# Pairing experts j and j+16, and summing each token's lower-block row ahead of the last scatter

## What is computed

```
def hier_moe(h, ...):                       # h: RMSNorm(x), 1088 x 1024
    pg = softmax(h @ w_rg + b_rg);  p_grp, g_sel = top_k(pg, 1)       # one of 4 groups
    le = einsum('nd,gde->nge', h, w_re) + b_re, of group g_sel        # 8 experts in it
    pe = softmax(le);  top_p, top_i = top_k(pe, 2)
    gates = p_grp * (top_p / sum(top_p));  eid = g_sel * 8 + top_i    # 2 of 32 experts
    y[token] += gate * (silu(xb @ w_eg[e]) * (xb @ w_eu[e])) @ w_ed[e]
x = x + hier_moe(rms_norm(x));  y_out = rms_norm(x)
```

## Time and profile before

| | |
|---|---|
| Time, median of 3 runs | 1012.75 us (1012.13 to 1013.37) |
| The profiled execution: its own time | 1013.96 us |
| Its span, first to last instruction | 1012.2 us |
| TensorE busy | 928.2 us (92%) |
| VectorE busy | 840.0 us (83%) |
| ScalarE (ACT) busy | 584.7 us (58%) |
| GpSimd (POOL) busy | 158.8 us (16%) |
| TensorE clock granted, mean | 0.962 |
| HBM read, written | 259.33 MB, 31.38 MB |

### The profile page before, as it was taken

The page is one execution under the profiler, slowest core; times in us unless marked ns, Lnnn a source line. Parts: engine busy times, 40 slices in busy tenths (PEclk is TensorE's granted clock), DMA queues, the critical chain, the costliest instruction groups (busy, mean ns, idle before and its releaser), DMA issues.

```text
span 1012.2 us, 13964 instructions
## 1 busy us (share of the span) xinstructions
PE 928.2 (92%) x4691; PEld 794.1 (78%) x4691; DVE 840.0 (83%) x932; ACT 584.7 (58%) x559; POOL 158.8 (16%) x201
## 2 busy tenths in 40 slices
PE   5999999968999988999999999999999999999900
PEld 5999988857888787788888888888888888888700
DVE  6489997897677676999989898988989898998658
ACT  7311101495232143778788787878878787887432
POOL 1000000000000021222122222212222221222100
PEclk9999999989999978999999999999999999999955
DMA  9421241321323257999999999999999999999776
GB/s 276 121 62 42 65 132 53 133 109 57 135 97 112 86 209 291 317 411 378 387 392 383 397 384 412 391 390 387 384 399 374 395 377 382 387 382 392 275 300 239
DMA packets 70954, 275.69 MB, mean 272 GB/s; under 512 B 16799, under 2 KB 31647, under 8 KB 45257
## 3 DMA queue, kind: packets, MB, share of 16 engines
q1 hardware_dynamic: 61129, 257.41, 67.6%
q0 software_dynamic: 9792, 17.85, 4.6%
HBM read 259.33 MB, written 31.38 MB: 287 GB/s over the span
## 4 chain that ended last, share of the span: by engine, by line
PE 86%; DVE 6%; DMA 3%; issue 2%; ACT 2%; SPq 0%; POOLq 0%; POOL 0%; DVEq 0%; ACTq 0%
PE ps L1163 11%; PE ps L1165 11%; PE ps L1164 11%; PE ps L1182 6%; PE ps L1180 6%; PE ps L1181 6%; PE ps L894 5%; PE ps L895 5%; PE ps L896 5%; PE ps L938 3%; PE ps L1052 3%; PE ps L1054 3%; PE ps L1053 3%; PE ps L1135 3%; DVE arena L1754 2%
## 5 line engine op out<-in xcount | busy, mean ns | idle before, releaser
L1663 DVE TENSOR_TENSOR big<-arena,big 128x2048 fp32r<-128x2048 f32 x128 | 287.1, 2285 | 0.0
L786 ACT ACTIVATE big<-arena 128x2048 fp32r<-128x2048 f32 x128 | 238.1, 1909 | 3.1 <-PE ps L1165 1.4
L1163 PE MATMUL ps<-big,ring 128*128 128x512 f32 x508 | 201.1, 396 | 2.3 <-DVE big L1663 2.3
L1165 PE MATMUL ps<-big,ring 128*128 128x512 f32 x508 | 198.1, 390 | 0.0
L1164 PE MATMUL ps<-big,ring 128*128 128x512 f32 x508 | 197.6, 389 | 0.0
L1663 DVE TENSOR_TENSOR slot_tail<-arena,slot_tail 128x2048 fp32r<-128x2048 f32 x62 | 139.1, 2285 | 0.0
L786 ACT ACTIVATE slot_tail<-arena 128x2048 fp32r<-128x2048 f32 x62 | 115.4, 1918 | 0.0
L1163 PEld LDWEIGHTS ps<-big,ring 128*128 128x128 f32 x508 | 95.4, 188 | 21.7 <-DVE big L1663 3.2
L1165 PEld LDWEIGHTS ps<-big,ring 128*128 128x128 f32 x508 | 95.4, 188 | 20.3
L1164 PEld LDWEIGHTS ps<-big,ring 128*128 128x128 f32 x508 | 95.5, 188 | 18.7
L1180 PE MATMUL ps<-slot_tail,hTr 128*128 128x512 f32 x248 | 99.2, 400 | 0.0
(11 more groups left out here) (251 smaller groups left out, 1424.4 us busy)
## 6 DMA issues: line engine op xcount, KB each, us to landing
arena<-in_w_eg SPq DMA_DIRECT2D x64, 1024.0 KB, 7.9
arena<-in_w_eu SPq DMA_DIRECT2D x64, 1024.0 KB, 9.1
arena<-in_w_ed SPq DMA_DIRECT2D x64, 1024.0 KB, 9.5
arena<-in_x_prompt SPq DMA_DIRECT2D x16, 512.0 KB, 5.1
arena<-y_scratch SPq DMA_DIRECT2D x8, 1024.0 KB, 11.3
arena<-in_w_in SPq DMA_DIRECT2D x12, 512.0 KB, 4.0
arena<-in_conv_band SPq DMA_DIRECT2D x8, 576.0 KB, 4.6
arena<-in_w_out SPq DMA_DIRECT2D x8, 512.0 KB, 5.2
```

The costliest lines, as they stand in the source:

```text
L786: act.activation(we_h[n % SLOTS], raw[n % RAWS], ACT.Copy).then_inc(high_done, 1)
L1163: pe.matmul(out, part_h[b][:, k, :], wh[:, i, :], start=(k == 0), stop=False)
L1165: ins = pe.matmul(out, part_l[b][:, k, :], wh[:, i, :], start=False, stop=(k == KD - 1))
L1663: dve.tensor_tensor(we_l[n % SLOTS], raw[n % RAWS], we_h[n % SLOTS].bitcast(F32), ALU.subtract).then_inc(low_done, 1)
```

## The change

Experts are paired j and j+16: block 2j holds expert j, block 2j+1 expert j+16. The router's weights and biases come from the host as two arrays with columns in block order, and are loaded in two transfers. A token's first row (k = 0) is now that of its lower block, its second row that of the higher one; e_top remembers which block had the larger logit, and the gates are swapped where that is not the first. The gates are worked out behind the last pair's second hidden product. At the end SP loads x2 tiles and first rows as raw slots come free during the last pair, once pair 14 has been scattered; VectorE adds first rows to x2 (add_first) ahead of all combines; second rows are loaded behind the last scatter, 512 KB per tile. ACT's scratch output lies in PSUM, and its table for the root is loaded before it waits.

```diff
+        PLACE = (2, 3, 4, 5, 0, 1, 6, 7, 8)
+        x_in = [arena[:, 2 * p * D:(2 * p + 1) * D] for p in PLACE]
+        y_first = [arena[:, (2 * p + 1) * D:(2 * p + 2) * D] for p in PLACE]
+        y_second = [arena[:, (2 * NT + 1 + s) * D:(2 * NT + 2 + s) * D] for s in range(FB)]
+        junk_f = banks(5, 2)
...
+            sp.dma_start(w_rt[:, :, :], w_router.rearrange("(p k) n -> p k n", p=P)).then_inc(consts_in, 16)
+            sp.dma_start(b_rt[:, :], b_router.partition_broadcast(P)).then_inc(consts_in, 16)
...
             def weights(j, first=False):
-                e = {b: 2 * j + b for b in (-1, 0, 1)}
+                e = {-1: j - 1 + E // 2, 0: j, 1: j + E // 2}
...
+            first_there = sp.value_load(eob[0:1, OVERFLOW + 2:OVERFLOW + 3], min_val=16 * PAIRS, max_val=16 * MAX_PAIRS + 16)
+            ahead = sp.value_load(eob[0:1, OVERFLOW + 3:OVERFLOW + 4], min_val=NP * PAIRS, max_val=NP * MAX_PAIRS + len(LAST))
+            for t in range(4):
+                sp.wait_ge(low_done, ahead + SLOTS + PLACE[t] + 1)
+                load_x2(t)
+            sp.wait_ge(scat[0], first_there)
+            sp.wait_ge(scat[1], first_there)
+            for t in range(4):
+                load_first(t)
+            for t in (4, 5):
+                sp.wait_ge(low_done, over(n_pairs - 1, NP - 2 + PLACE[t]))
+                load_x2(t)
+                load_first(t)
+            sp.wait_ge(piece_used, ahead + NP)
             sp.dma_start(gf_bc, norm_f_g.partition_broadcast(P)).then_inc(gf_in, 16)
-            sp.wait_ge(scat[0], 16 * n_pairs + 16)
-            sp.wait_ge(scat[1], 16 * n_pairs + 16)
+            for t in range(6, NT):
+                load_x2(t)
+                load_first(t)
+            for b in range(2):
+                sp.wait_ge(gath[b], 16 * n_pairs + 16)
+                sp.wait_ge(scat[b], 16 * n_pairs + 16)
             for t in range(FB):
-                load_y2(t)
+                load_second(t)
...
             over_loop(act, over_body)
+            act.activation(warm[:, :], eps[:, :], ACT.Sqrt)
...
-                step(dve.tensor_copy(eid[0:r, t, :], topi[0:r, 1, 0:2]))
+                dve.tensor_copy(e_top[0:r, t:t + 1], topi[0:r, 1, 0:1])
+                step(dve.tensor_copy(pair[0:r, :], topi[0:r, 1, 0:2]))
+                dve.tensor_tensor(eid[0:r, t, 0:1], pair[0:r, 0:1], pair[0:r, 1:2], ALU.min)
+                step(dve.tensor_tensor(eid[0:r, t, 1:2], pair[0:r, 0:1], pair[0:r, 1:2], ALU.max))
...
+                dve.memset(to_next[:, 0:E:2], float(E // 2))
+                step(dve.memset(to_next[:, 1:E:2], 1.0 - E // 2))
+                step(dve.tensor_tensor(cmp_[:, :, :], cmp_[:, :, :], to_next.unsqueeze(1).to_broadcast([1, OVERFLOW, E]),
+                                       ALU.mult))
                 step(dve.tensor_reduce(eob_f[:, 0:OVERFLOW], cmp_[:, :, :], AX_X, ALU.add))
-                step(dve.tensor_scalar(eob_f[:, 0:OVERFLOW], eob_f[:, 0:OVERFLOW], float(E - 1), None, ALU.min))
...
+                pairs, first_rows, ahead = (eob_f[:, OVERFLOW + i:OVERFLOW + i + 1] for i in range(3))
+                step(dve.tensor_scalar(first_rows, pairs, float(PAIRS), None, ALU.is_gt))
+                step(dve.tensor_scalar(ahead, first_rows, float(len(LAST)), None, ALU.mult))
+                step(dve.scalar_tensor_tensor(ahead, pairs, float(NP), ahead, ALU.mult, ALU.add))
+                step(dve.tensor_tensor(first_rows, first_rows, pairs, ALU.add))
+                step(dve.tensor_scalar(first_rows, first_rows, 16.0, None, ALU.mult))
                 step(dve.memset(eob[:, 0:1], E - 1))
-                dve.tensor_copy(eob[:, 1:OVERFLOW + 2], eob_f[:, 0:OVERFLOW + 1]).then_inc(plan_done, 1)
+                dve.tensor_copy(eob[:, 1:OVERFLOW + 4], eob_f[:, 0:OVERFLOW + 3]).then_inc(plan_done, 1)
+            def set_gates():
...
+                step(dve.tensor_tensor(e_top[:, :], e_top[:, :], eid[:, :, 0], ALU.not_equal))
+                step(dve.tensor_tensor(gtmp[:, :, :], gates[:, :, :], e_top[:, :].unsqueeze(1).to_broadcast([P, 2, NT]),
+                                       ALU.mult))
+                step(dve.tensor_tensor(gates[:, :, :], gates[:, :, :], gtmp[:, :, :], ALU.subtract))
+                dve.tensor_tensor(gates[:, 0, :], gates[:, 0, :], gtmp[:, 1, :], ALU.add)
+                step(dve.tensor_tensor(gates[:, 1, :], gates[:, 1, :], gtmp[:, 0, :], ALU.add))
...
             hidden(PAIRS - 1, 1)
+            set_gates()
             hidden_low(PAIRS - 1, 1)
             over_loop(dve, over_body)
+            def add_first(t):
+                r = ROWS[t]
+                dve.wait_ge(f_x[t], 32)
+                dve.scalar_tensor_tensor(x_in[t][0:r, :], y_first[t][0:r, :], gates[0:r, 0, t:t + 1], x_in[t][0:r, :],
+                                         ALU.mult, ALU.add).then_inc(f_half, 1)
...
+            for t in range(NT):
+                add_first(t)
             for t in range(NT):
                 combine(t)
```

More of the change, by code:

```diff
@@ L62, in trunk_kernel @@
     LB = GROUPS + E
[L63 removed]
+    assert SEQ == 2 * BANK and 2 * IW + PS <= SEQ - PS and SEQ < T and NC + DPOOL // P == KD and NG == NC == 4 and KD == 8 and KF == 4 and PER == 8 and GROUPS == 4 and NBLK % 2 == 0
     VW = CS + SEQ + CS + DEC
@@ L192, in trunk_kernel @@
         FB = 6
[L193 to L196, removed]
+        PLACE = (2, 3, 4, 5, 0, 1, 6, 7, 8)
+        x_in = [arena[:, 2 * p * D:(2 * p + 1) * D] for p in PLACE]
+        y_first = [arena[:, (2 * p + 1) * D:(2 * p + 2) * D] for p in PLACE]
+        gf_bc = arena[:, 2 * NT * D:(2 * NT + 1) * D]
+        y_second = [arena[:, (2 * NT + 1 + s) * D:(2 * NT + 2 + s) * D] for s in range(FB)]
+        assert RAWS * HP == 12 * D
         ident = sb("ident", [P, P])
@@ L229, in trunk_kernel @@
         edif = sb("edif", [P, NT])
+        pair = sb("pair", [P, 2])
+        e_top = sb("e_top", [P, NT])
         gates = sb("gates", [P, 2, NT])
@@ L1745, in _ @@
             hidden(PAIRS - 1, 1)
+            set_gates()
             hidden_low(PAIRS - 1, 1)
             over_loop(dve, over_body)
+            def add_first(t):
+                r = ROWS[t]
+                dve.wait_ge(f_x[t], 32)
+                dve.scalar_tensor_tensor(x_in[t][0:r, :], y_first[t][0:r, :], gates[0:r, 0, t:t + 1], x_in[t][0:r, :],
+                                         ALU.mult, ALU.add).then_inc(f_half, 1)
             def combine(t):
                 r, s = ROWS[t], t % FB
-                dve.wait_ge(f_x[t], 16)
+                dve.wait_ge(f_half, t + 1)
                 dve.wait_ge(f_in[s], 16 * (t // FB + 1))
-                for k in range(2):
-                    dve.scalar_tensor_tensor(x_in[t][0:r, :], y_in[s][0:r, k * D:(k + 1) * D], gates[0:r, k, t:t + 1],
-                                             x_in[t][0:r, :], ALU.mult, ALU.add).then_inc(f_acc, 1)
-                    dve.wait_ge(f_acc, 2 * t + k + 1)
+                dve.scalar_tensor_tensor(x_in[t][0:r, :], y_second[s][0:r, :], gates[0:r, 1, t:t + 1], x_in[t][0:r, :],
+                                         ALU.mult, ALU.add).then_inc(f_acc, 1)
+                dve.wait_ge(f_acc, t + 1)
             def final(t):
@@ L1794, in _ @@
             for g in range(GROUPS):
-                pool.memset(grp[:, g * PER:(g + 1) * PER], float(g))
+                first = g % 2 * 2 * PER + g // 2
+                pool.memset(grp[:, first:first + 2 * PER - 1:2], float(g))
             for i in range(PS):
@@ L1932, in phased_bias, with by_block, router_weights, router_bias @@
     return np.ascontiguousarray(np.tile(conv_dw_b[256:].reshape(-1, 32).T, (4, 1)))
+def by_block(of_experts):
+    import numpy as np
+    n = of_experts.shape[-1]
+    return of_experts[..., [i // 2 + n // 2 * (i % 2) for i in range(n)]]
+def router_weights(w_rg, w_re):
+    import numpy as np
+    w = np.moveaxis(w_re, 0, 1).reshape(w_re.shape[1], -1)
+    return np.ascontiguousarray(np.concatenate([w_rg, by_block(w)], axis=1))
+def router_bias(b_rg, b_re):
+    import numpy as np
+    return np.ascontiguousarray(np.concatenate([b_rg, by_block(b_re.reshape(-1))]))
 _INS = ["x_prompt", "x_sample", "state_pool", "state_conv", "norm1_g", "w_in", "pool_lin", "pool_scale", "conv_dw", "conv_band",
-        "conv_dw_b", "conv_b_ph", "conv_ln_g", "conv_ln_b", "w_out", "b_out", "norm2_g", "w_rg", "b_rg", "w_re", "b_re", "w_eg",
+        "conv_dw_b", "conv_b_ph", "conv_ln_g", "conv_ln_b", "w_out", "b_out", "norm2_g", "w_router", "b_router", "w_eg",
         "w_eu", "w_ed", "norm_f_g"]
@@ L1951 @@
             a = phased_bias(np.asarray(inputs["conv_dw_b"])[0])
+        elif name == "w_router":
+            a = router_weights(np.asarray(inputs["w_rg"])[0], np.asarray(inputs["w_re"])[0])
+        elif name == "b_router":
+            a = router_bias(np.asarray(inputs["b_rg"])[0], np.asarray(inputs["b_re"])[0])
         else:
```

48 lines of the change are left out of this document (22 added, 26 removed).

## The result

| | before | after |
|---|---|---|
| Time, median (lowest to highest), 4 runs each | 1012.92 us (1012.13 to 1013.37) | 1006.96 us (1005.93 to 1008.37) |
| Ratio, 95% interval | | 0.9947 [0.9935, 0.9959] |
| The profiled execution: its own time, span | 1013.96, 1012.2 us | 1007.59, 1005.6 us |
| VectorE busy | 840.0 us | 844.0 us |
| TensorE clock granted, mean | 0.962 | 0.968 |

The kernel became faster by 6.0 us, where 8.7 were forecast. Single executions of one kernel differ by some microseconds, and one reason that the profiles show is TensorE's clock at the first gather of expert rows: in the profiled execution of before it had fallen there (granted clock 0.77 in 375 to 390 us), in that of after it had not (1.00).

What follows compares the result with a forecast made beforehand. TensorE was taken to bound the expert loop, and VectorE's sums behind the last scatter and load the tail. Terms -11.7 + 2.4 + 0.6 = -8.7 gave 1004.0 us from a median of 1012.75, range 1001.0 to 1009.0.

Steps and rivals of the forecast that it cites:

- The sums: Tail behind the last pair: nine of eighteen VectorE sums, 1.30 us each, move ahead of the last scatter; -11.7 us.
- The start of the tail: Tile 0's combine, behind nine first sums, last scatter and one load, starts at 974.5 instead of 972.14; +2.4 us, bounds 972.2 to 979.7.
- the scatter's route: Start of the tail by the last scatter: landed at 970.9, its half-size load behind it, tile 0 ready at 974.4 to 975.6.
- third route: Start of the tail by SP's load queue: 19 units of 1.37 us from 946.9, through at 972.9.
- POOL beside the sums: Last block: POOL's index copy and descriptor writing are slowed by VectorE's first sums running beside them; +0.8 and +1.3 us.
- The load queue's route: Start of the tail by SP's loads: tile 8's first sum ends at 974.2, a second row lands at 974.3.
- The first pair: overflow_plan ahead of low 9: gates and clamp leave, a multiply and small steps come, on TensorE's path; +0.6 us, bounds 0 to 1.2.
- The edits at nothing: Moved gates, routing additions, fewer constant loads and pairing addresses lie under existing idle or busy time; no cost.
- (a): Rival: all transfers hide in the tail, so VectorE's floor of 972.2 decides; 1001.8 us, chance 0.12.
- (b): Rival: the last scatter is starved, landing after 10.1 us, and the tail starts at 979.7; 1009.2 us, chance 0.07.
- (c): Rival: first rows are held back until the last scatter, all eighteen sums stay behind it; 1013.4 us, chance 0.04.
- (d): Rival: experts 32 MB apart are read more slowly, so TensorE waits for weights in every pair; 1020 us, chance 0.05.

Runs made afterwards that it cites:

- the version with all first rows behind: Changed kernel, but all first rows loaded behind the last scatter and summed just ahead of each tile's combine; 1013.09 us, ratio 1.0006 to the kernel before.
- the changed kernel with the plan early: Changed kernel with overflow_plan moved from between low 8 and low 9 to behind rows_low(j, 1) of the first pair; 1003.26 us, ratio 0.9907.

## Why the prediction was right, and where its terms were off

- **The sums**, -11.7: measured -11.70, with one sum per tile in a period of 2.71 us.
- **The start of the tail**, +2.4: measured +6.2, inside the bounds but far from the value taken. The step that was mis-sized is the scatter's route: "The scatter issued at 956.0, among loads, landed after 4.8 instead of 3.20; the last scatter will now meet loads too, so 1.6 more." It was 6.4 more (9.59). The loads beside the scatter of 956.0 ran out while it was under way (q1 moved 0.40 MB in 957 to 958 of that trace, 0.23 in 958 to 959, 0.02 in 959 to 960, and the scatter's packets moved from 958 on); the right rows were the scatters of the weight stream, 10.1, which had been set aside for a rival because "this queue" ends. By the third route of the same section it ends at 972.9, eight microseconds behind the scatter's issue: the two routes were worked out apart, and the first did not use what the second said.
- **POOL beside the sums**, +0.8 and +1.3: the copy took 0.18 as before, the descriptors 1.15 instead of 0.98, +0.17 together. The two terms did not come, which hid part of the error in the scatter.
- **The load queue's route**: near in the trace's time, but too short as well. The last first row was forecast to land at 972.9; it was issued at 955.6 and landed 18.2 later, at 973.8, in an execution that was 1.07 ahead by then. From the first landing (942.03 + 3.5 = 945.5) the 19 units took 1.49 us each, not 1.37. The sum of tile 8 ended at 975.10, 13.12 behind POOL's copy: this route by itself makes +4.0, and the scatter's the remaining 2.17. A second row did not land right behind it, as the forecast had it, but 4.55 us behind a scatter that landed at 972.55.
- **The first pair**, +0.6: the plan took 408.64 - 404.65 = 3.99 instead of 3.50, and the wait 2.15 instead of 1.69, so the instructions were sized well (+0.5, and a wait near the 2.3 named). What was not foreseen is that the clock can fall behind that wait, 1.6 us more in this execution. The profile is nevertheless 1.07 ahead at the last block, since it was 2.95 ahead at the end of TensorE's wait of 0.66 for an earlier low part (402.60 against 405.55): 0.52 of that stood at the last ranks (367.04 against 367.56), the first gather ended TensorE's wait 1.43 earlier (382.26 against 383.69), and from there to the rows of block 1 before took 1.49 longer (7.20 against 5.71) at the fallen clock. Over many executions such differences even out: +0.6 [-0.4, +1.6] in the version with all first rows behind. Why the clock falls in some executions at the first gather and not in others is open: in the six profiles with the fall TensorE had waited 2.86 to 4.08 us for it, in the seven without 0.91 to 3.11.
- **The edits at nothing** cost nothing: the gates end at 951.6, under an idle time of 2.77 that remains ahead of 954.37, the last count ends at 366.38, before TensorE's last ranks at 367.04, and the pairs follow in 35.39 us.
- **The rivals.** (a), all transfers hide: no, VectorE waited 3.91, 0.28, 0.22 and 2.17 us for rows. (b), the last scatter starved: its mechanism is what happened, 9.59 of its 10.1 us; its 1009.2 was too high by 1.4 at the start of the tail (+7.6 against +6.2, 0.8 of it the POOL copy's delay) and by 1.7 ahead of the last block (+0.6 against -1.07). (c) and (d): no; seven of the nine sums lie ahead of the scatter's landing, and the loop is untouched.

In sum -11.7 + 6.2 - 1.07 = -6.6 on the profiled spans, in place of -8.7. The sign rested on the sums, and these were exact. That the time is within the range is in part luck: the start of the tail came by the way of (b), which had a chance of 0.07, 3.8 later than the value taken, and 1.7 of that was given back ahead of the last copy by a difference between two executions that the forecast did not know.

## What to carry to other kernels

Work that is pulled ahead of a latency-bound step is not free if it brings its transfers along: here nine sums saved 11.7 us and the loads for them gave 6.2 back, because the loads took until 973.8 and the scatter that met a filled load queue landed 6 us later, no later with two more loads in the queue. When two routes to one time are worked out, put the result of each into the other before taking the later of them. And a short stall of TensorE can cost more than its length, through the clock that follows it; moving 4 us of VectorE's work from in front of TensorE into a gap it already had was worth 3.7 us, beside the 6.0 of the change itself.

## What was not expected of the hardware

- A scatter's 144 packets stood still for some 4 us behind loads and then took 5 us beside them, against 1 to 2 us and 2 us alone (the queue views above).
- POOL's index copy beside VectorE's sums took 0.18 to 0.19 us in eight profiles and 0.94 and 0.91 in two. In the eight it began 2.4 us behind the first sum, where the third begins (six sums in 7.26, 1.21 each); in the two, 4.0 us behind it, within the fourth, which had 0.86 left (4 x 1.21 - 3.98). POOL's timeline of the changed kernel with the plan early, whose sums began at 958.58:

```profile
962.56 0.94 POOL L1940 COPY cur<-s_idx 128x1 uint32<-128x1 uint32 x1 [7.73 <-ACT arena L835]
964.29 1.21 POOL L1916 DMA_INDIRECT y_scratch<-arena,cur  x1 [0.80 <-POOL cur L1940]
```

  So the term of 0.8 was real in those two executions and missing in the others by the moment at which the copy came, and that moment was 1.6 us later because these are the two profiles in which TensorE's clock fell in the last block. Descriptor writing took 1.15 to 1.21 beside sums and 0.98 without; no run shows it held up for a whole sum.
- The Trainium skill (SBUF — State Buffer, section "SBUF: two separate sides") says that an instruction on the shared port pair keeps it until it ends and the other engine waits; for a VectorE instruction with two SBUF inputs it says so only against a GpSimd one that reads SBUF. The copies, which read s_idx there, agree with that, 0.94 and 0.18 by where in a sum they began. Its estimate in the prediction, 2.6 us for copy and descriptors, was not reached in any run: 0.17 to 1.0 was measured.
